# A halo loop that takes its rows in stream order and projects keys and values as tiles arrive

## The chip, the cores and the metric

The kernel runs on all eight cores of one Trainium2 chip. Each core has a TensorE (PE), a VectorE (DVE), a ScalarE (ACT), a GpSimd (POOL) and a SyncE (SP), which work through queues of their own and meet at semaphores. Times are device microseconds of the slowest core. A time is the median of several executions; a profile is one execution on the slowest core.

## What is computed

One decoder layer over 16384 positions of width 1024. Cut to what this change touches:

```python
h = rms_norm(x, g_pre_mix)
proj = h @ w_in                       # q, k, v (768 each), u (256), gates (2048)
q = apply_rope(q); k = apply_rope(k)
# head groups: (window, dilation) = (128, 1), (512, 4), (2048, 16)
outs, lses = [dilated_window_attention(q_g, k_g, v_g, window, dilation) ...]
o_attn = sum(softmax(lses) * outs)
y_pool = multiscale_pool(u, w_pool_mix, pool_scale)   # trailing means over 2, 4, 8, 16
x = x + rms_norm((gate_a * (o_attn @ w_proj_attn) + gate_p * (y_pool @ w_proj_pool)) @ w_out)
x = x + rms_norm((silu(a) * b) @ w_down)              # [a, b] = rms_norm(x) @ w_gate_up
```

In a group of dilation r the positions fall into r streams (position mod r). A query sees the keys of its stream in its own block and in the block before.

## The kernel before

A core owns 2048 positions (16 own tiles of 128, `xo`) and also reads the 2048 positions ahead of them, the **halo** (16 tiles, `xh`), because attention of dilation 16 looks back that far. From the halo the kernel needs keys and values of group 2 (dilation 16) for all 2048 positions, of group 1 for the last 512, of group 0 for the last 128, and u for the last 16.

A tile of x goes through four steps: `t_sq` (ACT squares and sums the row; POOL or ACT and DVE make the reciprocal root), `t_xs` (ACT or DVE scales the row into one of three buffers `xsb`), `t_tr` (PE transposes it in eight 128x128 pieces, DVE writes it out times the gain, into `hTh` for the halo and `hT` for own tiles). A tick of the halo loop (`s_`) squares tile s_, transposes tile s_-3 and scales tile s_-2. `x_load` brings tiles into ten buffers through SP's queue; a load waits for the scaling that frees its buffer. Own tiles have `own_tick`, which does the same steps one tick apart.

`rope_unit` projects keys or queries of a pair of heads for n columns (`proj_fm`: eight matmuls), copies the result to `qb` on ACT, and leaves the rest to the next unit's `rope_flush`: one matmul with `rotm`, two DVE products with the cos and sin tables, one POOL sum into `kT` or `qT`. The tables come by `load_tables`, 512 columns at a time, into two buffers. `v_block` projects 128 positions to values (eight matmuls) and evacuates them. Weights are loaded by POOL's queue (`wload`, `wplan`) and cast to bf16 on the way.

The halo loop has K units of group 2 alone, two for each quarter of the halo (512 positions, `k_halo`). After the loop, in this order: the last quarter's K units, 16 V blocks of group 2 (`v_halo`; stream r reads every 16th column of `hTh`), K and V of group 1, of group 0, and u of the last 16, with an `own_tick` between every few. Then four own blocks of 512 positions follow, each of 12 rope units, with five own ticks in each of the first two and u units in the last two. Then attention starts (line 769 on), and later the gates, the output projection and the FFN.

The code is run straight through by Python; each engine's queue has the order in which the calls stand. There is no scheduler.

## Time and profile before

| | us |
|---|---|
| median of 3 runs | 1005.5 (1005.11 to 1005.79) |
| the profiled execution | 1003.87 |
| its span, slowest core | 1002.3 (cores 998.6 to 1002.3) |
| PE busy | 926.7 (92%) |
| DVE, ACT, POOL busy | 395.6, 343.0, 327.0 |
| mean granted TensorE clock | 0.979 on either die |

The span is the time from the first to the last instruction on the core; the execution has 1.6 us around it. Engine shares are means over stages with different limits, so the stretch that a change touches has to be read by itself, by windows and by the timeline.

### The profile page before, as it was taken

The page shows a single profiled execution, that of the slowest core. Times are in us where ns is not written, and L with a number is a line of the kernel's source. Part 1 is how long each engine was busy: PE and PEld are TensorE (multiplying, and loading weights), DVE is VectorE, ACT ScalarE, POOL GpSimd, SP SyncE. Part 2 cuts the span into 40 slices and gives each one's busy share as a digit, 9 for nine tenths or more (in the row PEclk, how much of TensorE's full clock was granted, in tenths as well). Part 3 has the DMA queues.
Part 4 walks back from the last instruction along what each step waited for, and adds up shares of the span by engine and source line. Part 5 has one row for each costly group of instructions (what it writes and reads, how often), then busy time and mean ns, then how long its engine had stood idle before and what let it go on. Part 6 is the DMA issues. An engine that isn't in the chain of part 4 may idle for free.

```text
span 1002.3 us, 15188 instructions; the slowest of 8 cores (998.6 to 1002.3 us)
## 1 busy us (share of the span) xinstructions
PE 926.7 (92%) x5532; PEld 465.2 (46%) x5532; DVE 395.6 (39%) x556; ACT 343.0 (34%) x580; POOL 327.0 (33%) x318
## 2 busy tenths in 40 slices
PE   1559999999897999999998999999999999999993
PEld 1238554456564444444454444444444444444441
DVE  2466786548887332233687211121112211221111
ACT  4427663349777322223664111110111111111100
POOL 3462787763400333333465111111322000001231
PEclk9779999999999999999999999999999999999997
DMA  8989320000050171112978767663234444430332
GB/s 230 253 186 238 82 64 22 1 1 2 2 86 2 54 115 29 36 22 52 304 273 185 126 111 122 107 118 75 104 126 118 73 84 68 80 63 1 127 110 79
DMA packets 32586, 98.50 MB, mean 98 GB/s; under 512 B 4224, under 2 KB 4224, under 8 KB 32512
## 3 DMA queue, kind: packets, MB, share of 16 engines
q0 software_dynamic: 15296, 41.92, 25.2%
q1 hardware_dynamic: 17072, 55.58, 16.6%
q8 instruction: 45, 0.74, 0.3%
q14 instruction: 29, 0.24, 0.1%
q10 hardware_dynamic: 144, 0.03, 0.0%
HBM read 122.64 MB, written 16.78 MB: 139 GB/s over the span
## 4 chain that ended last, share of the span: by engine, by line
PE 87%; issue 3%; DVE 3%; DMA 2%; ACT 2%; POOL 2%; SPq 0%; DVEq 0%; ACTq 0%; POOLq 0%
PE ps L1194 15%; PE ps L1160 15%; PE ps L1163 14%; PE ps L438 12%; PE ps L934 6%; PE ps L937 6%; PE ps L997 6%; PE ps L518 5%; DMA xst<-xh 2%; PE ps L420 2%; PE ps L944 1%; PE ps L941 1%; PE ps L482 1%; PE ps L791 1%; PE ps L769 1%
## 5 line engine op out<-in xcount | busy, mean ns | idle before, releaser
L1163 PE MATMUL ps<-hT,wgu 128*128 128x512 bf16 x672 | 158.7, 379 | 0.0
L1160 PE MATMUL ps<-hT,wgu 128*128 128x512 bf16 x672 | 158.7, 379 | 0.0
L1194 PE MATMUL ps<-wdn,ffT 128*128 128x512 bf16 x704 | 152.3, 379 | 0.4 <-DMA wdn<-wdn 0.4
L1175 DVE TENSOR_TENSOR ffT<-ps,sa 128x512 bf16<-128x512 f32 x88 | 60.7, 690 | 222.5 <-PE ps L1163 222.5
L1174 ACT ACTIVATE sa<-ps 128x512 f32<-128x512 f32 x88 | 52.5, 597 | 238.8 <-PE ps L1160 238.7
L1194 PEld LDWEIGHTS ps<-wdn,ffT 128*128 128x128 bf16 x704 | 68.8, 98 | 83.7 <-issue 0.8
L1163 PEld LDWEIGHTS ps<-hT,wgu 128*128 128x128 bf16 x672 | 65.7, 98 | 79.3
L1160 PEld LDWEIGHTS ps<-hT,wgu 128*128 128x128 bf16 x672 | 65.6, 98 | 78.6
L74 POOL DMA_DIRECT2D wgu<-wgu x42 | 22.5, 537 | 234.6 <-PE ps L1163 227.5
L438 PE MATMUL ps<-hT,wqk 128*128 128x512 bf16 x384 | 90.5, 379 | 1.2 <-DVE t L485 1.2
L1010 POOL TENSOR_TENSOR x1b<-tb,xin 128x1024 f32<-128x1024 f32 x31 | 72.8, 2348 | 54.4 <-DVE tb L1005 29.6
L956 POOL TENSOR_TENSOR mT<-m,m 128x512 bf16<-128x512 f32 x32 | 40.6, 1268 | 142.9 <-DVE m L951 142.9
L498 POOL TENSOR_TENSOR kT<-t,t2b 128x512 bf16<-128x512 f32 (+1 forms) x36 | 65.6, 1826 | 43.5 <-DVE t2b L487 39.8
L359 ACT ACTIVATE junk<-ps 128x1024 bf16<-128x1024 f32 x31 | 31.5, 1017 | 138.0 <-PE ps L1194 130.8
L1005 DVE SCALAR_TENSOR_TENSOR tb<-ps,rsA,gfin 128x1024 f32<-128x1024 f32 x15 | 19.3, 1284 | 129.5 <-POOL rsA L343 129.5
L508 ACT ACTIVATE qb<-ps 128x512 bf16<-128x512 f32 (+1 forms) x60 | 35.0, 584 | 83.8 <-PE ps L438 82.1
L934 PE MATMUL ps<-hT,wgs 128*128 128x512 bf16 x256 | 62.2, 387 | 0.0
L937 PE MATMUL ps<-hT,wgs 128*128 128x512 bf16 x256 | 60.8, 380 | 0.0
L950 DVE TENSOR_TENSOR m<-ps,sga 128x512 f32<-128x512 f32 x32 | 22.1, 692 | 95.1 <-PE ps L941 91.7
L420 PE MATMUL ps<-ident,xsb 128*128 128x128 bf16 x256 | 23.3, 246 | 38.9 <-ACT xsb L407 20.9
L773 ACT ACTIVATE PT<-ps 128x1024 bf16<-128x1024 f32 x48 | 54.5, 1143 | 12.1 <-PE ps L769 12.1
L438 PEld LDWEIGHTS ps<-hT,wqk 128*128 128x128 bf16 x384 | 37.1, 98 | 44.0 <-issue 1.3
(119 smaller groups left out, 1200.7 us busy)
## 6 DMA issues: line engine op xcount, KB each, us to landing
wgu<-wgu POOLq DMA_DIRECT2D x42, 512.0 KB, 5.2
xst<-xh SPq DMA_DIRECT2D x16, 512.0 KB, 19.1
xin<-xo SPq DMA_DIRECT2D x16, 512.0 KB, 5.4
x1s<-x1b SPq DMA_DIRECT2D x16, 512.0 KB, 3.7
xin<-x1s SPq DMA_DIRECT2D x16, 512.0 KB, 3.9
out<-x1b SPq DMA_DIRECT2D x15, 512.0 KB, 2.9
xst<-xo SPq DMA_DIRECT2D x12, 512.0 KB, 8.6
wdn<-wdn POOLq DMA_DIRECT2D x22, 256.0 KB, 6.0
```

Source lines behind the costliest of these rows:

```text
L438: ev = pe.op(lambda e, k=k: e.matmul(ps[:, bank, 0:n], lhsT=wfn(k), rhs=rhsfn(k), start=(k == 0), stop=(k == 7)), signal=(k == 7))
L498: ev_o = pool.op(lambda e: e.tensor_tensor(out=dst, in0=i0, in1=i1, op=ALU.add), waits=[ev_t1, ev_t2])
L773: ev_e = act.op(lambda e: e.activation(out=PT[k3][:, :, :], in_=ps[:, b0:b0 + 2, :], func=AF.Exp, scale=0.125), waits=[ev, pt_free[k3]])
L934: e1 = pe.op(lambda e, k=k, wb=wb, b1=b1, tok=tok: e.matmul(ps[:, b1, :], lhsT=wgs[wb][:, 0, k, :], rhs=hT[:, k, tok], start=(k == 0), sto ...
L937: e2 = pe.op(lambda e, k=k, wb=wb, b2=b2, tok=tok: e.matmul(ps[:, b2, :], lhsT=wgs[wb][:, 1, k, :], rhs=hT[:, k, tok], start=(k == 0), sto ...
L997: ev = pe.op(lambda e, k=k, hf=hf, pr_=pr_: e.matmul(ps[:, pr_[0] + hf, :], lhsT=mT[:, k, i * 128:(i + 1) * 128], rhs=wout[:, k, hf * 512: ...
L1010: ev_o = pool.op(lambda e: e.tensor_tensor(out=outbuf[:, :], in0=tb[b][:, :], in1=xres[:, :], op=ALU.add), waits=[ev_t, ev_xres, out_free])
L1160: e1 = pe.op(lambda e, k=k, wbuf=wbuf, ba=ba, tok=tok: e.matmul(ps[:, ba, :], lhsT=wbuf[:, 0, k, :], rhs=hT[:, k, tok], start=(k == 0), st ...
L1163: e2 = pe.op(lambda e, k=k, wbuf=wbuf, bb=bb, tok=tok: e.matmul(ps[:, bb, :], lhsT=wbuf[:, 1, k, :], rhs=hT[:, k, tok], start=(k == 0), st ...
L1174: es = act.op(lambda e, ub=ub, ba=ba: e.activation(out=sa[ub][:, :], in_=ps[:, ba, :], func=AF.Silu), waits=[e1, sa_free[ub]])
L1175: ef = dve.op(lambda e, ub=ub, bb=bb, j=j, b=b: e.tensor_tensor(out=ffT[:, j, b * 512:(b + 1) * 512], in0=ps[:, bb, :], in1=sa[ub][:, :], ...
L1194: ev = pe.op(lambda e, j=j, h2=h2, pr_=pr_, il=il: e.matmul(ps[:, pr_[0] + h2, :], lhsT=ffT[:, j, il * 128:(il + 1) * 128], rhs=wdn[:, j, ...
```

## The change

**Halo rows by streams.** The host hands over the halo's 2048 rows permuted, so that tile i holds the 128 positions of stream i (position mod 16 = i), and permutes the cos and sin columns alike. A tile is then one V block of group 2, and four tiles are a K quarter that lies in contiguous runs (`k_stream`, forms -1 to -3 in `rope_flush`).

**Values eight ticks behind.** `v_stream(s_ - 8)` stands in each tick from 8 to 23. The halo's transposed tiles live in a ring of eight, `hTs`, instead of `hTh`; the write of tile i waits for the V block of tile i-8 and for the K units that read its half.

**Last columns kept as runs.** `t_hc` copies the last 32 columns of each tile (its share of the last 512 positions) into `hTc` on ACT. From it come group 1's K and V; `hTd` (last 128) and `hTu` (last 16) are copied from it by ACT after the loop. The keys of those blocks stand in another order, so the first block's masks have their rows permuted alike, and there are four instead of three; a further 512 columns of tables in that order are loaded.

**Four table buffers** instead of two.

**Own ticks.** Own tiles 0 to 3 run in the ticks 16 to 22 of the loop, with the V blocks. Tiles 4 to 15 run in blocks 0 and 1, eight ticks and seven.

**The halo's rest inside the first own block.** K and V of group 1 after unit 3 of block 0, K and V of group 0 after unit 5, u of the last 16 inside block 1. The order of units in blocks 0 to 2 is 10, 11, 8, 9, 6, 7, 4, 5, 2, 3, 0, 1.

**Small ones.** In a tick the scaling stands ahead of the transpose; half of the scalings are on ACT instead of a third; weight loads of wk1 and later stand three ticks and more later; ACT's table is loaded by a one-column square at the start and ACT no longer waits for `cpk`; POOL no longer waits for the end of the halo before the masks.

```diff
@@ t_tr
-        dst, c0 = (hTh, i * 128) if i < NTH else (hT, (i - NTH) * 128)
+        dst, c0 = (hTs, i % 8 * 128) if i < NTH else (hT, (i - NTH) * 128)
...
+            ew = [str_pe.get(i - 8), str_pe.get(("k", i // 4 - 2)), ev_hc.get(i - 8)]
...
+    def t_hc(i):
+        c0, c1 = i % 8 * 128, 128 * (i % 4) + 32 * (i // 4)
+        ev_hc[i] = act.op(lambda e: e.activation(out=hTc[:, :, c1:c1 + 32], in_=hTs[:, :, c0 + 96:c0 + 128], func=AF.Copy), waits=[hev[i]])
...
+    def v_stream(r):
+        c0 = r % 8 * 128
+        v_block(wvr, 2, lambda k: hTs[:, k, c0:c0 + 128], blk_idx(2, r, 0), extra_waits=[wld_ev["wv2"], hev[r]], evac="act" if r % 4 == 0 else "dve")
+        str_pe[r] = pe.last()
...
@@ halo loop
-    for s_ in range(NTH + 3):
+    for s_ in range(NTH + 8):
...
+            if i == 11:
+                tab_own = load_tables(3, HT, 12)
+            if i == 13:
+                tab_n = load_tables(2, HT + T, 4)
+        if 0 <= s_ - 3 < NTH:
+            t_tr(s_ - 3)
+        if 0 <= s_ - 4 < NTH:
+            t_hc(s_ - 4)
+        if 0 <= s_ - 8 < NTH:
+            v_stream(s_ - 8)
+        if 7 <= s_ < 21 and s_ % 4 in (3, 0):
+            k_stream((s_ - 7) // 4, (s_ + 1) % 4)
...
+        if 18 <= s_ < 22:
...
+            x_load(NTH + s_ - 14)
+        if 16 <= s_ < 23:
+            own_tick(0)
+    ev_hd = act.op(lambda e: e.activation(out=hTd[:, :, :].rearrange("p k (r j) -> p k r j", j=8), in_=hTc[:, :, :].rearrange("p k (r j) -> p k r j", j=32)[:, :, :, 24:32],
+                                          func=AF.Copy), waits=[ev_hc[NTH - 1]])
...
@@ own blocks
+    tick_at = {0: (1, 3, 4, 5, 6, 7, 8, 9), 1: (0, 2, 4, 6, 8, 9, 10)}
...
-        order = (6, 10, 7, 11, 8, 9, 0, 4, 1, 5, 2, 3) if b < 3 else (10, 4, 11, 5, 8, 2, 9, 3, 6, 0, 7, 1)
+        order = (10, 11, 8, 9, 6, 7, 4, 5, 2, 3, 0, 1) if b < 3 else (10, 4, 11, 5, 8, 2, 9, 3, 6, 0, 7, 1)
...
+            if b == 0 and n == 3:
+                for pr in range(2):
+                    k_halo(1, pr)
+                for r in range(4):
+                    v_halo(1, r, "dve")
```

How PE's queue changes. Before, in the halo loop from tile 12 on and behind it (the transposes write `hTh`, L438 with `wqk` is a K unit, L482 the product with `rotm`, L518 a V block):

```order
L420 MATMUL ps<-ident_43,xsb_34_76 128x128 x8
L438 MATMUL ps<-hTh_81,wqk_62 128x512 x8
L420 MATMUL ps<-ident_43,xsb_35_77 128x128 x8
L438 MATMUL ps<-hTh_81,wqk_62 128x512 x8
L482 MATMUL ps<-qb_45_87,rotm_44 128x512
L420 MATMUL ps<-ident_43,xsb_36_78 128x128 x8
L482 MATMUL ps<-qb_46_88,rotm_44 128x512
L420 MATMUL ps<-ident_43,xsb_34_76 128x128 x8
L438 MATMUL ps<-hTh_81,wqk_62 128x512 x16
L482 MATMUL ps<-qb_45_87,rotm_44 128x512
L518 MATMUL ps<-wvr_63,hTh_81 128x256 x16
```

Now, from tile 12 on in the loop (L424 is the transpose, L449 the K unit, L538 the V block, L493 the product with `rotm`):

```order
L424 MATMUL ps<-ident_43,xsb_35_77 128x128 x8
L538 MATMUL ps<-wvr_64,hTs_82 128x256 x8
L449 MATMUL ps<-hTs_82,wqk_63 128x512 x8
L424 MATMUL ps<-ident_43,xsb_36_78 128x128 x8
L538 MATMUL ps<-wvr_64,hTs_82 128x256 x8
L449 MATMUL ps<-hTs_82,wqk_63 128x512 x8
L493 MATMUL ps<-qb_52_94,rotm_44 128x512
L424 MATMUL ps<-ident_43,xsb_37_79 128x128 x8
L538 MATMUL ps<-wvr_64,hTs_82 128x256 x8
L493 MATMUL ps<-qb_53_95,rotm_44 128x512
```

Every tick has a V block behind its transpose, which before stood behind the loop.

ACT's queue in own block 0. Before, units without and with a tick take turns (L508 copies qb; L407 scales, L390 squares, L396 takes the root of an own tile):

```order
L508 ACTIVATE qb_45_87<-ps 128x512
L508 ACTIVATE qb_46_88<-ps 128x512
L407 ACTIVATE xsb_36_78<-hTf_82,rsA_50 128x1024
L390 ACTIVATE junk_38_80,ssA_48<-xst_25_67 128x1024
L396 ACTIVATE msA_49<-ssA_48 128x1
L508 ACTIVATE qb_45_87<-ps 128x512
L508 ACTIVATE qb_46_88<-ps 128x512
L407 ACTIVATE xsb_34_76<-xst_24_66,rsA_50 128x1024
```

Now, from unit 6 of block 0 on (L528 copies qb, L411 scales, L394 squares, L400 takes the root):

```order
L528 ACTIVATE qb_52_94<-ps 128x512
L411 ACTIVATE xsb_36_78<-hTf_85,rsA_51 128x1024
L394 ACTIVATE junk_38_80,ssA_49<-xst_25_67 128x1024
L400 ACTIVATE msA_50<-ssA_49 128x1
L528 ACTIVATE qb_53_95<-ps 128x512
L411 ACTIVATE xsb_37_79<-hTf_85,rsA_51 128x1024
L394 ACTIVATE junk_39_81,ssA_49<-xst_26_68 128x1024
L400 ACTIVATE msA_50<-ssA_49 128x1
L528 ACTIVATE qb_52_94<-ps 128x512
```

Each unit there has a scaling, a square and a root behind it, and the next copy of qb stands behind these.

## Rows read from the trace of the kernel before

**Rows 1.** The page, the span in 40 equal slices, busy tenths and granted clock
```profile
PE   1559999999897999999998999999999999999993
...
PEclk9779999999999999999999999999999999999997
```

**Rows 2.** Windows: stretch, its length, busy us per engine (instructions), clock, DMA share, GB/s
```profile
0.00:72.09 72.09, 29.40 (x183) 16.61 (x183) 33.89 (x41) 28.58 (x45) 33.67 (x57) 0.86 0.87 222
72.09:106.70 34.61, 32.98 (x286) 26.41 (x286) 21.80 (x47) 21.74 (x40) 11.84 (x10) 0.94 0.76 195
106.70:218.40 111.70, 111.63 (x578) 53.19 (x579) 74.89 (x118) 50.13 (x86) 86.75 (x53) 1.00 0.14 38
...
40.00:72.09 32.09, 17.96 (x109) 9.78 (x109) 19.10 (x22) 11.26 (x19) 18.96 (x25) 0.71 0.83 180
```

**Rows 3.** Waits from 0 to 72 us: us in total, times, longest
```profile
PE ps L420 <- ACT xsb L407: 20.9, 4, 13.7
...
PE ps L420 <- DVE xsb L409: 18.0, 8, 3.1
```

**Rows 4.** Timeline: start, duration, engine, line, operation, count, [idle before, releaser]
```profile
28.65 3.38 PE L438 MATMUL ps<-hTh,wqk 128*128 128x512 bf16 x8
...
32.31 1.89 PE L438 MATMUL ps<-hTh,wqk 128*128 128x512 bf16 x8
...
39.31 1.06 ACT L390 ACTIVATE junk<-xst 128x1024 bf16<-128x1024 f32 x1 [2.34 <-DMA xst<-xh]
...
47.69 0.60 ACT L508 ACTIVATE qb<-ps 128x512 bf16<-128x512 f32 x1 [5.98 <-PE ps L438]
...
56.79 1.04 ACT L390 ACTIVATE junk<-xst 128x1024 bf16<-128x1024 f32 x1
```

**Rows 5.** Timeline of SP's queue, issues of the loads of x
```profile
14.34 16.91 SPq L74 DMA_DIRECT2D xst<-xh  x6
...
54.83 0.33 SPq L74 DMA_DIRECT2D xst<-xo  x1
```

**Rows 6.** DMA: GB/s in 40 slices of 0 to 70 us, then queues of 0 to 130
```profile
GB/s 0 86 213 248 275 298 260 256 229 174 300 261 290 294 307 274 240 286 352 339 283 323 288 246 249 162 235 105 50 29 110 201 115 238 171 149 272 229 234 232
...
q1 hardware_dynamic: 6704, 19.40, 49.0%
q0 software_dynamic: 3200, 5.74, 26.8%
```

**Rows 7.** Timeline, 86 to 90 us, V blocks, a transpose, and an own tick on ACT
```profile
86.59 2.79 PE L518 MATMUL ps<-wvr,hTh 128*128 128x256 bf16 x24
...
87.00 1.15 ACT L407 ACTIVATE xsb<-xst,rsA 128x1024 bf16<-128x1024 f32 x1
...
88.06 1.04 ACT L390 ACTIVATE junk<-hTf 128x1024 bf16<-128x1024 f32 x1
...
89.22 0.61 PE L420 MATMUL ps<-ident,xsb 128*128 128x128 bf16 x8
89.29 0.20 ACT L396 ACTIVATE msA<-ssA 128x1 f32<-128x1 f32 x1
...
89.67 2.79 PE L518 MATMUL ps<-wvr,hTh 128*128 128x256 bf16 x24
```

**Rows 8.** Groups by line from 0 to 235 us: busy, mean ns, idle before
```profile
L487 DVE TENSOR_TENSOR t2b<-ps,sin 128x512 f32<-128x512 f32 x58 | 40.0, 689 | 28.6 <-PE ps L482 27.7
...
L425 DVE TENSOR_TENSOR hTh<-ps,cpk 128x1024 bf16<-128x1024 bf16 x16 | 19.5, 1223 | 35.7 <-PE ps L420 35.7
...
L524 DVE CAST vA<-ps 128x256 bf16<-128x256 f32 x21 | 8.8, 421 | 5.7 <-PE ps L518 5.7
...
L409 DVE TENSOR_SCALAR xsb<-xst,rsA 128x1024 bf16<-128x1024 f32 x10 | 7.4, 744 | 0.0
```

**Rows 9.** Timeline of PE in own block 0
```profile
112.82 1.89 PE L438 MATMUL ps<-hT,wqk 128*128 128x512 bf16 x8
...
114.76 0.61 PE L420 MATMUL ps<-ident,xsb 128*128 128x128 bf16 x8
```

More of the change, by code:

```diff
@@ L257, in build_program @@
     rotm = P.sb("rotm", [128, 128], BF16, take(256))
-    masks = P.sb("masks", [128, 3, 512], BF16, take(3072))
+    masks = P.sb("masks", [128, 4, 512], BF16, take(4096))
+    hTu = P.sb("hTu", [128, 8, 16], BF16, take(256))
     cpk = P.sb("cpk", [128, 52], F32, take(208))
@@ L366, in build_program @@
     tr_ring = Ring([0, 1])
-    hTh = P.sb("hTh", [128, 8, 2048], BF16, R_Q)
+    hTs = P.sb("hTs", [128, 8, 1024], BF16, R_Q)
+    hTc = P.sb("hTc", [128, 8, 512], BF16, R_Q + 16 * KB)
+    hTd = P.sb("hTd", [128, 8, 128], BF16, R_X + 14 * KB)
+    str_pe = {}
+    ev_hc = {}
     NTH = HT // 128
@@ new lines, in v_stream, with k_halo @@
+    def v_stream(r):
+        c0 = r % 8 * 128
+        v_block(wvr, 2, lambda k: hTs[:, k, c0:c0 + 128], blk_idx(2, r, 0), extra_waits=[wld_ev["wv2"], hev[r]], evac="act" if r % 4 == 0 else "dve")
+        str_pe[r] = pe.last()
+    def k_halo(g, pr):
+        if g:
+            dst = kT[1][:, pr, :].rearrange("p (s L) -> p s L", s=4)[:, :, 0:128]
+            rope_unit(8 + pr, hTc, 512, -2, tab_n, dst, [wld_ev["wk1"], ev_hc[NTH - 1]])
+        else:
+            rope_unit(6 + pr, hTd, 128, -3, tab_n, kT[0][:, pr, 0:128], [wld_ev["wk0"], ev_hd])
@@ new lines, in v_halo, with own_tick @@
+    def v_halo(g, r, evac):
+        fn = (lambda k: hTc[:, k, 128 * r:128 * r + 128]) if g else (lambda k: hTd[:, k, :])
+        v_block(wvr, g, fn, blk_idx(g, r, 0), extra_waits=[wld_ev["wv%d" % g], ev_hc[NTH - 1], ev_hd], evac=evac)
+    own = NTH
+    own_k = [0, 0]
+    def own_tick(batch):
+        k = own_k[batch]
+        own_k[batch] += 1
+        lo, hi = (4, NT) if batch else (0, 4)
+        k += lo
+        if lo <= k - 1 < hi:
+            t_rc(own + k - 1)
+        if lo <= k - 3 < hi:
+            t_tr(own + k - 3)
+        if lo <= k - 2 < hi:
+            n = k - 2
+            t_xs(own + n, n % 2 == 0 or n > 3)
+            if 8 <= n < 12:
+                x_load(own + n + 4)
+        if batch and k < 8:
+            x_load(own + k + 4)
+        if k < hi:
+            t_sq(own + k)
@@ L544, in build_program @@
+    warm = act.op(lambda e: e.activation(out=msA[:, 0:1], in_=nhalf[:, :], func=AF.Square), waits=[ev_ms1])
+    for i in range(6):
         x_load(i)
     tab_h = [load_tables(0, 0, 2)]
-    for i in range(4, NXB):
+    for i in range(6, NXB):
         x_load(i)
     tab_h.append(load_tables(1, 512, 2))
-    wplan = {0: [lambda: load_wk(2)], 1: [lambda: wload("rotm", rotm[:, :], rotm_d[:, :])], 4: [lambda: load_wv(2)],
-             8: [lambda: load_wk(1)], 10: [lambda: load_wk(0)], 12: [lambda: load_wv(1)], 14: [lambda: load_wv(0)],
-             16: [lambda: load_wq(0)], 17: [lambda: load_wq(2)], 18: [lambda: load_wq(1)]}
@@ L624, in build_program @@
-    for f in k0:
-        f()
-    v_halo(0, 0, "dve")
-    own_tick()
-    rope_flush()
-    for c in range(2):
-        k_, bank, ev = proj_fm(lambda k, c=c: wu_t[c][:, k, :], lambda k: hTh[:, k, 2032:2048], 16, [wld_ev["wu"]])
-        ev2 = dve.op(lambda e, c=c, bank=bank: e.tensor_copy(out=uh[:, c, :], in_=ps[:, bank, 0:16]), waits=[ev])
+            if i == 11:
[4 more added lines that the diff above has]
+            t_tr(s_ - 3)
@@ new lines, in build_program @@
+        if 0 <= s_ - 4 < NTH:
[4 more added lines that the diff above has]
+            k_stream((s_ - 7) // 4, (s_ + 1) % 4)
+        if s_ >= 9 and s_ % 4 == 1 and s_ <= 21:
+            rope_flush()
+            if s_ <= 13:
+                tab_h.append(load_tables((s_ - 9) // 4, 1024 + 128 * (s_ - 9), 2))
+        if 18 <= s_ < 22:
+            if s_ == 18:
+                xst_free[NXB:] = [[xsc[t] for t in range(6, NTH)]] * 4
+            x_load(NTH + s_ - 14)
@@ new lines, in build_program @@
+        if 16 <= s_ < 23:
+            own_tick(0)
+    ev_hd = act.op(lambda e: e.activation(out=hTd[:, :, :].rearrange("p k (r j) -> p k r j", j=8), in_=hTc[:, :, :].rearrange("p k (r j) -> p k r j", j=32)[:, :, :, 24:32],
+                                          func=AF.Copy), waits=[ev_hc[NTH - 1]])
+    ev_hu = act.op(lambda e: e.activation(out=hTu[:, :, :].rearrange("p k (q s) -> p k s q", s=4), in_=hTc[:, :, 31:512:32].rearrange("p k (s q) -> p k s q", s=4),
+                                          func=AF.Copy), waits=[ev_hc[NTH - 1]])
@@ L632, in build_program, with u_halo @@
+    def u_halo(c):
+        k_, bank, ev = proj_fm(lambda k: wu_t[c][:, k, :], lambda k: hTu[:, k, :], 16, [wld_ev["wu"], ev_hu])
+        ev2 = dve.op(lambda e: e.tensor_copy(out=uh[:, c, :], in_=ps[:, bank, 0:16]), waits=[ev])
         pj_ring.release(k_, ev2)
         bank_free[bank] = ev2
-    ev_hTh = pe.last()
-    pool.wait(ev_hTh)
     L = 2064
@@ L776, in att_scores @@
         bank_free[b1] = ev_e
-        mv = 2 if g == 2 else (1 if half == 0 and (g == 1 or s_ == 0) else 0)
+        mv = 2 if g == 2 else ((3 if g else 1) if half == 0 and (g or s_ == 0) else 0)
         att_ev[u] = dve.op(lambda e: e.tensor_tensor(out=PT[k3][:, :, :], in0=PT[k3][:, :, :], in1=masks[:, mv, :].unsqueeze(1).to_broadcast([128, 2, 512]),
```

137 lines of the change are left out of this document (54 added, 83 removed).

## The prediction

> **What bounds the kernel now.** I read the page first. TensorE is busy 92% of the span, and the only long hollow stretch is at the start: the PE line opens with 1, 5, 5 tenths while PEclk stands at 9, 7, 7 [rows 1]. The windows say where it ends. Up to 72.1 us PE is busy 29.4 us, with DMA at 0.87; from 72.1 to 106.7 us it is busy 32.98 of 34.61; from 106.7 to 218.4 us, where attention starts, 111.63 of 111.70 us at clock 1.00 [rows 2]. So after 72.1 us the time to 218.4 us is PE work and almost nothing else, and only two things shorten it: to start this dense stretch earlier, or to do part of its work in the hollow before it. Behind 218.4 us nothing is edited that costs time (a fourth mask of the same shape, same instructions), so I carry the end of this phase straight to the end of the kernel.
>
> The hollow has two causes. Until about 39 us the loads lead: ACT's square of halo tile 10 waits for its transfer (39.31) [rows 4]. Behind it no square waits for a transfer; the square of tile 15 runs at 56.79, five tiles in 17.5 us, 3.5 us each. What paces these is the hand-over: PE's transposes wait 20.9 us for xsb from ACT and 18.0 us from DVE [rows 3]. The K projection of a quarter runs its first eight matmuls at the lower clock (3.38 us, the next eight 1.89 us), ACT waits up to 5.98 us for its result (47.69), and the next tile's scaling stands behind that [rows 4]. Loads meanwhile run dry: SP issues the last halo load by 31.2 us and the first own tile only at 54.83 [rows 5], and GB/s falls to 105, 50, 29 around 50 us [rows 6].
>
> **The change, part by part.**
>
> *(a) Sixteen V blocks of dilation 16 move from behind 72.1 us into the halo loop.* The halo rows now come in stream order, so each tile is a complete V block and can be projected eight ticks after its load. Eight matmuls cost 2.63/3 = 0.88 us (86.59 to 89.22, 24 of them) [rows 7]; sixteen are 14.0 us off the dense stretch. The last K quarter (2 units) and own tiles 0 to 3 (4 transposes) also come before the first own block. A unit is 1.94 us (112.82 to 114.76), a transpose 0.45 us (89.22 to 89.67, where the next matmuls start) [rows 7, 9]: 3.9 + 1.8. The halo's rest (K1 2 units 3.9, K0 about 1.3 by its quarter of the columns, 5 V blocks 4.4, the 16-column u pair about 0.5) moves inside block 0 and stays PE work.
>
> *(b) What is left behind the first own matmul.* The stretch 106.7 to 218.4 us keeps its 111.6 us; it holds 10 transposes of own tiles and will hold 12, +0.9; plus 3.9 + 1.3 + 4.4 + 0.5. Sum 122.6 us. The end of the phase is S + 122.6 + stalls, where S is the start of own block 0. Break-even is S = 218.4 - 122.6 - 4 = 92.
>
> *(c) S by the ticks.* A tick holds a square, half an ACT and half a DVE scaling, one transpose with its evacuation, one V block, and on two ticks of four a K unit. DVE: 1.22 + 0.74/2 + 0.42 x 3/4 + 0.69 (half of the two products with the tables, alike) = 2.6 us [rows 8]. ACT: square 1.05 to 1.23, half of 1.06 [rows 7], half of a 0.60 us copy of qb [rows 4], a quarter of 0.42, and the new copy of 32 columns x 8 into hTc. No row shows that copy; it has 256 elements a partition, like the 0.42 us evacuation [rows 8], and a quarter of the 1.15 us scaling [rows 7] would be 0.29. I take 0.4: 2.4 us. PE at the upper clock: 0.45 + 0.88 + 1.94/2 = 2.3 us; at the lower one twice that. So about 2.6 us of the busiest engine, and 2.8 with hand-overs; what was a chain (scale, transpose, K, copy, next scale) has its values three to eight ticks ahead now, which is why I don't take the 3.5 us. Tile 10 cannot come before about 39 us (same bytes ahead of it). Tick 19, nine later, is at 39.3 + 25.2 = 64.5 (at 2.6: 63; at 3.5: 71). Ticks 19 and 20 hold K and V, 3.3 us each, 21 to 23 about 1.5 each: S = 75.6, say **76**.
>
> *(d) S by the loads.* Own tile 3 is needed at tick 19. In the first 130 us SP's queue took 49.0% for 19.40 MB, 3.28 us per MB, and POOL's 26.8% for 5.74 MB, 6.07 us per MB [rows 6]. Ahead of or beside own tile 3 now stand 20 tiles and 5 pairs of tables (13.1 MB, 43 us) and five weight groups (2.6 MB, 16 us): 59 us of engine time, which from a start at 2 to 3 us and with small holes is 62 to 68 us. The loads and the ticks meet; own tiles are issued at tick 12 instead of at 54.83, which fills the hole at 50 us. Two pairs of tables more (own block 0, the extra 512 columns) are in this; the extra pair costs 1.7 us of DMA and stands behind own tile 3.
>
> *(e) Block 0.* Eight ticks for own tiles 4 to 11 stand here, where before five were in a block. A unit with its tick costs ACT 0.60 for qb [rows 4], 1.06 for the scaling, 1.23 for the square and 0.20 for the root, 3.1 us [rows 7], and PE 2.39 us [rows 9]; the transposed product of each unit waits for ACT's qb, so PE can't run ahead. Seven such units in a row are 4.9 us, less what the K0, V0 insert and the first unit's slack give back (about 2.5 us). ACT's two new copies (hTd, 1024 elements, about 1.1 us; hTu) stand before the block's first qb and lie under its first 1.7 us of matmuls. The squares of own tiles 4 to 7 queue behind transfers that are issued at tick 18; if late, ACT stops, and with it qb and PE. I allow **4 us** of stalls in all (1.6 us in the stretch from 72.1 to 106.7 us now [rows 2]).
>
> *(f) Order inside a block* (K2, K1, K0, Q2, Q1, Q0): POOL's heavier sums come four in a row. The last block of before already has such a row and PE has no gap there [rows 2]: nothing. *(g)* The early table load and the dropped wait for cpk start the first square some 2 us sooner, but tile 10 is bound by the loads: nothing.
>
> **Sum.** 76 + 122.6 + 4 = 202.6 us against 218.4: 15.8 us. The profiled execution has span 1002.3 and took 1003.87, 1.6 us under the median of 1005.5. Less 16: span 986.3, that execution 987.9, and on the scale of the median **989.5 us**.
>
> **A rule weighed.** From 40 to 72.1 us the granted clock was 0.71, with PE busy 17.96 of 32.09 us, and from 106.7 us on it was 1.00 [rows 2]. Work in the loop from the first K on is 16 transposes, 16 V, 8 K units = 7.2 + 14.1 + 15.6 = 36.9 us at the upper level; at a mean of 0.71 it would be 52 us, from 28.65 to about 81, five us later than my S. The Trainium skill, "TensorE: Matmul & The Clock Gate", section "What's actually happening", says the default state is throttled and activity releases it. By it the denser loop keeps the upper clock and S stays 76; by the row's mean S would be 81. The second eight matmuls of a quarter at 1.89 us [rows 4] bear the rule out for dense stretches.
>
> **Rivals.**
> 1. *PE stays at the lower clock through the loop (slower).* Gaps between ticks are small but regular. 36.9 us of work then cost 74 us: S = 102, end 102 + 122.6 + 3 = 227.6, 9 us late: 1014.7. It decides against the change from S = 92 on. For it: the lower clock in two slices. Against: PE would be some 80% busy there (36.9 of 47 us) instead of 56%, and the second unit of each pair ran at the upper level even now.
> 2. *Own tiles land late.* If two more weight groups (6.4 us) go ahead and the engines are at 0.87 [rows 2], own tile 3 lands at (59 + 6.4)/0.87 + 2.5 = 78, S = 85, gain 7: 998.5. For it: SP's queue holds everything in order, a table load that waits holds own tiles behind it.
> 3. *ACT sets block 0.* The full 4.9 us, and nearly as much again for squares that wait for tiles 4 to 7: stalls 9, gain 11: 994.5.
> 4. *Better.* Full clock, ticks at 2.6, no stall: S = 70, end 70 + 122.6 + 1 = 193.6, gain 25: 980.7.
> 5. *Nothing gained*: the ticks take 3.5 us and more and rivals 2 and 3 come together, S + stalls near 96: 1005.5.
>
> **How the numbers follow.** Forecast (gain 13 to 19) 0.45, rival 2 0.17, rival 3 0.17, rival 4 0.12, rival 5 0.03, rival 1 0.06. About 0.2% (2 us) is what a measurement of this kernel can tell from no change. Faster 0.91, same 0.03, slower 0.06. The range 982 to 999 takes in rivals 2 and 3 whole and half of rival 4, and leaves out about 0.15.
>
> **What would show it.** Right: the stream's V matmuls stand between 33 and 75 us with the later ones at the upper clock; PE busy in 40 to 72 us rises from about 18 to 25 us or more; the first matmul on own columns at 76 (70 to 82); the phase before attention ends near 203; from there on all as before. Step (c) fails if the squares of tiles 11 to 15 are more than 3.2 us apart; (d) if ACT waits for own tiles at ticks 16 to 19; (e) if PE has more than 5 us of gaps between S and S + 35, behind qb. The whole fails if V blocks in the loop run at twice 0.88 us throughout, or if the first own matmul is later than 92 us.

## The result, and the profile after

| | before | after |
|---|---|---|
| median | 1005.3 us | 997.9 us (996.3 to 1000.6) |
| ratio to before | | 0.9926, 95% interval 0.9903 to 0.9949 |
| span of the profiled execution, slowest core | 1002.3 | 999.0 |
| first matmul of own block 0, median of the cores | (104.8, behind the halo's rest) | 80.5 (79.7 to 81.9) |
| first attention score, median of the cores | 219.1 (217.8 to 221.0) | 211.4 (209.2 to 212.9) |

The kernel is faster by 0.7%, 7.4 us at the medians, where 16 us were forecast. The sign and the mechanism were right; the size was half. A second measurement of the same kernel (e0_again below) gave 996.0 and the ratio 0.9903, a gain of 10 us. Medians, here and below, leave out the executions in which the cores of one die ran at a lower granted clock and took longer.

In what follows, **S** is the start of own block 0's first matmul, **phase** the time from there to the first score matmul of attention, and **tail** the time from there to the end of the core's span. All of them count from the core's own first instruction. On the slowest core of before the first score stands at 221.0, 2.6 us behind the end of the dense stretch in [rows 2], so a phase without stalls is 122.6 + 2.6 = 125.2 us. The kernel after on its slowest core, 7, is S 81.7, phase 131.2, tail 786.1.

The page of after, its two lines of busy tenths and clock, to be laid beside [rows 1]:

```profile
PE   1779899998897999999998999999999999999993
...
PEclk9999999999998999999999999999999999999997
```

The opening 1, 5, 5 has become 1, 7, 7, and the clock's dip to 7 in the second and third slice is gone. The same in windows (columns as in [rows 2]):

```profile
40.00:64.00 24.00, 20.46 (x178) 14.17 (x176) 21.80 (x32) 18.88 (x38) 16.14 (x26) 1.00 0.76 178
64.00:82.00 18.00, 12.86 (x84) 8.15 (x85) 10.95 (x19) 6.93 (x14) 8.14 (x13) 0.81 1.03 254
82.00:116.90 34.90, 32.11 (x196) 17.27 (x194) 20.99 (x39) 18.60 (x36) 18.88 (x16) 0.95 0.62 144
116.90:210.00 93.10, 92.49 (x490) 43.90 (x489) 62.07 (x98) 42.13 (x72) 70.22 (x40) 1.00 0.11 35
...
40.00:72.09 32.09, 25.77 (x211) 16.98 (x209) 23.95 (x37) 21.33 (x43) 17.61 (x28) 1.00 0.83 191
```

Against the same 32 us in [rows 2], PE is busy 25.77 us instead of 17.96, at clock 1.00 instead of 0.71. But from 64 to 82 us there is a new hollow: 5.1 us of PE idle, clock 0.81, and the DMA share is 1.03, the most of any of these windows.

ACT's timeline in that hollow (core 7; squares at L394, of halo tile 15 at 52.35, of own tiles 0 to 3 at 59.25, 60.90, 69.02, 72.68):

```profile
52.35 1.05 ACT L394 ACTIVATE junk<-xst 128x1024 bf16<-128x1024 f32 x1
...
60.90 1.04 ACT L394 ACTIVATE junk<-xst 128x1024 bf16<-128x1024 f32 x1
...
69.02 1.06 ACT L394 ACTIVATE junk<-xst 128x1024 bf16<-128x1024 f32 x1 [4.71 <-DMA xst<-xo]
...
72.68 1.06 ACT L394 ACTIVATE junk<-xst 128x1024 bf16<-128x1024 f32 x1 [1.42 <-DMA xst<-xo]
```

Up to 52.35 the stream runs as forecast (53.3 by the sum). Then own tiles 2 and 3 are not there. Two short windows show that the DMA engines had time for them earlier (share 0.33 and 0.35, the number before the last):

```profile
39.00:43.00 4.00, 2.86 (x33) 2.42 (x33) 4.00 (x6) 3.90 (x9) 3.07 (x4) 1.00 0.33 105
43.00:47.00 4.00, 4.00 (x31) 2.49 (x29) 3.79 (x6) 2.30 (x5) 3.32 (x8) 1.00 0.35 120
```

but SP's queue (issue time, duration) shows that the loads of own tiles 0 and 1, and then of 2 and 3, went out only behind this hole:

```profile
47.73 2.29 SPq L74 DMA_DIRECT2D xst<-xo  x2
50.07 0.42 SPq L74 DMA_DIRECT2D cos<-cost  x1
...
53.60 1.50 SPq L74 DMA_DIRECT2D xst<-xo  x2
```

Two operations that free buffers set these times, on ACT the scaling of halo tile 10 and on DVE a product with a table:

```profile
46.52 1.14 ACT L411 ACTIVATE xsb<-xst,rsA 128x1024 bf16<-128x1024 f32 x1
...
51.60 0.68 DVE L503 TENSOR_TENSOR t2b<-ps,sin 128x512 f32<-128x512 f32 x1
```

Own tile 0 takes the buffer of halo tile 10, and its load is issued when that scaling has ended (47.7 us). The loads of own tiles 2 and 3 stand in SP's queue behind a pair of tables, which is issued at 52.35, when the product has released its buffer. POOL's queue shows what stood beside them, five weight groups of 0.5 MB issued at 45 to 64 us:

```profile
45.44 1.16 POOL L74 DMA_DIRECT2D wqk<-wk  x2
51.69 1.16 POOL L74 DMA_DIRECT2D wqk<-wk  x2
56.39 0.62 POOL L74 DMA_DIRECT2D wvr<-wv  x1
61.41 0.57 POOL L74 DMA_DIRECT2D wvr<-wv  x1
64.36 1.10 POOL L74 DMA_DIRECT2D wqk<-wq  x2
```

PE's timeline, from the wait to the first own block, and then the place in block 0 with group 0's K and V (`hTd`):

```profile
73.04 1.01 PE L424 MATMUL ps<-ident,xsb 128*128 128x128 bf16 x8 [1.26 <-DVE xsb L413]
73.85 1.92 PE L538 MATMUL ps<-wvr,hTs 128*128 128x256 bf16 x8
...
81.68 3.61 PE L449 MATMUL ps<-hT,wqk 128*128 128x512 bf16 x16 [0.60 <-DVE hT L432]
...
102.86 0.38 PE L493 MATMUL ps<-qb,rotm 128*128 128x512 bf16 x1 [0.87 <-ACT qb L528]
...
105.40 0.22 PE L493 MATMUL ps<-qb,rotm 128*128 128x128 bf16 x1 [1.72 <-ACT qb L528]
105.63 1.51 PE L538 MATMUL ps<-wvr,hTd 128*128 128x256 bf16 x8
106.93 3.14 PE L449 MATMUL ps<-hT,wqk 128*128 128x512 bf16 x8
```

These waits are paid twice: behind them a transpose takes 1.01 us instead of 0.61, a V block 1.92 instead of 1.04, a K unit's eight matmuls 3.14 instead of 1.89, wholly or in part at the lower of TensorE's two clocks (1.2 instead of 2.4 GHz).

The third place is far behind the change, at the start of the output projection. The cores come in pairs (0 and 1, 2 and 3, and so on). In the kernel after, the one of a pair that begins the output projection later (each by the time since its own first instruction) has the longer tail in all four pairs: 785.1 against 780.0, 783.8 against 780.5, 783.8 against 780.8, 786.1 against 780.2 us. The waits of POOL there, from 455 to 520 us (us in total, times, longest), on core 7 and then on its partner 6:

```profile
POOL x1b L1045 <- DMA xin<-xo: 7.8, 2, 4.8
```
```profile
POOL x1b L1045 <- DMA xin<-xo: 2.9, 2, 1.6
```

`xin` are the rows of x that the output projection adds back (line 1045, one sum `x1b` on POOL for each of 16 tiles). On core 7 they come late: the third sum ends 23.2 us behind the core's first output projection matmul, on core 6 18.3 us, and the last one 77.2 against 74.1 us. PE on core 7 waits for the outcome at the start of the FFN, and then for the FFN's own `ffT`; on core 6 it has only the second wait:

```profile
527.67 0.61 PE L1096 MATMUL ps<-ident,xs 128*128 128x128 bf16 x8 [1.93 <-DVE xs L1084]
529.51 3.45 PE L1195 MATMUL ps<-hT,wgub 128*128 128x512 bf16 x8 [1.23 <-DVE ffT L1210]
```
```profile
523.83 1.89 PE L1195 MATMUL ps<-hT,wgub 128*128 128x512 bf16 x8 [1.08 <-DVE ffT L1210]
```

The matmuls behind the two waits take 3.45 us, those behind the single one 1.89. From its first output projection matmul to its first FFN matmul with weights loaded in the FFN itself (`wgu`; the first two groups are `wgub`) core 7 takes 81.3 us and core 6 76.6. I call this the **burst stretch**.

The tail of core 7, 786.1, is 4.8 us longer than the 781.3 of the slowest core of before. Of these, 2.4 us are in the burst stretch (81.3 against 78.9), 1.0 between the first score and the output projection, and 1.4 behind the stretch. Only the first part is followed up below; the causes of the other two are open.

### The profile page after: what moved, and what is told of

Read it like the earlier page. It is cut to its first block, busy times and chain, and to the rows that moved or that the text cites. A ratio compares the mean times of both kernels' runs of the same rounds, so it can differ in the third digit from the quotient of the medians.

```text
span 999.0 us, 15229 instructions; the slowest of 8 cores (989.2 to 999.0 us)
## 1 busy us (share of the span) xinstructions
PE 926.5 (93%) x5532; PEld 462.5 (46%) x5532; DVE 394.0 (39%) x552; ACT 350.3 (35%) x603; POOL 320.1 (32%) x318
## 4 chain that ended last, share of the span: by engine, by line
PE 80%; DMA 6%; ACT 4%; issue 4%; DVE 3%; POOL 2%; SPq 1%; DVEq 0%; ACTq 0%; POOLq 0%
PE ps L1229 15%; PE ps L1195 15%; PE ps L1198 15%; PE ps L449 10%; PE ps L969 6%; PE ps L972 6%; PE ps L538 5%; DMA xst<-xh 2%; DMA xin<-xo 2%; DMA xst<-xo 2%; PE ps L979 1%; PE ps L976 1%; PE ps L826 1%; PE ps L804 1%; POOL x1b L1045 1%
## 5 line engine op out<-in xcount | busy, mean ns | idle before, releaser
L449 PE MATMUL ps<-hT,wqk 128*128 128x512 bf16 x384 | 91.6, 383 | 0.6 <-DVE hT L432 0.6
L518 POOL TENSOR_TENSOR kT<-t,t2b 128x512 bf16<-128x512 f32 (+1 forms) x36 | 57.5, 1612 | 42.3 <-DVE t2b L503 36.9
L528 ACT ACTIVATE qb<-ps 128x512 bf16<-128x512 f32 (+1 forms) x60 | 34.9, 584 | 67.8 <-PE ps L449 61.3
L449 PEld LDWEIGHTS ps<-hT,wqk 128*128 128x128 bf16 x384 | 37.3, 99 | 43.6 <-issue 2.5
L1032 PE MATMUL ps<-wout,mT 128*128 128x512 bf16 x256 | 56.9, 379 | 0.0
```

What stands on the lines that cost most here:

```text
L449: ev = pe.op(lambda e, k=k: e.matmul(ps[:, bank, 0:n], lhsT=wfn(k), rhs=rhsfn(k), start=(k == 0), stop=(k == 7)), signal=(k == 7))
L518: ev_o = pool.op(lambda e: e.tensor_tensor(out=dst, in0=i0, in1=i1, op=ALU.add), waits=[ev_t1, ev_t2])
L1032: ev = pe.op(lambda e, k=k, hf=hf, pr_=pr_: e.matmul(ps[:, pr_[0] + hf, :], lhsT=mT[:, k, i * 128:(i + 1) * 128], rhs=wout[:, k, hf * 512: ...
```

## The experiments

All use the kernel after as their base, except e9. Ratios are to the kernel before on the same chip, where its median was between 1005.3 and 1006.5. S and attention start are medians over eight cores of one profile, the late tail is the mean over the four cores that begin the output projection later than their partner.

| run | median us | ratio (95% interval) | S | attention | late tail |
|---|---|---|---|---|---|
| before | 1005.3 | 1 | | 219.1 | 782.0 |
| after | 997.9 | 0.9926 (0.9903 to 0.9949) | 80.5 | 211.4 | 784.7 |
| e0_again | 996.0 | 0.9903 (0.9878 to 0.9927) | 79.8 | 210.1 | 782.0 |
| e1_weights_late | 991.9 | 0.9862 (0.9841 to 0.9884) | 75.6 | 206.4 | 782.8 |
| e2_v_one_eighth | 996.7 | 0.9908 (0.9885 to 0.9931) | 79.5 | 211.1 | 782.3 |
| e3_v_double | 997.7 | 0.9909 (0.9882 to 0.9936) | 82.2 | 212.2 | 783.5 |
| e4_ticks_off_k0 | 995.4 | 0.9902 (0.9877 to 0.9927) | 80.1 | 208.8 | 783.2 |
| e5_weights_and_ticks | 991.2 | 0.9861 (0.9838 to 0.9885) | 75.6 | 204.8 | 782.5 |
| e6_late_weights_v_eighth | 996.2 | 0.9898 (0.9873 to 0.9923) | 77.0 | 208.4 | 782.8 |
| e7_boot_later | 988.1 | 0.9819 (0.9799 to 0.9839) | 75.6 | 204.8 | 780.2 |
| e8_tables_late | 998.0 | 0.9913 (0.9891 to 0.9935) | 78.2 | 212.2 | 781.4 |
| e9_before_boot_later | 1003.9 | 0.9976 (0.9963 to 0.9989) | | 219.1 | 780.7 |
| e10_after_boot_later | 995.1 | 0.9883 (0.9864 to 0.9903) | 79.4 | 209.6 | 780.7 |
| e11_all_and_tables | 990.0 | 0.9831 (0.9809 to 0.9853) | 75.5 | 204.7 | 781.2 |

An interval is about 2.3 us to either side, so only differences of 3 us and more between two rows are to be read in time; smaller ones only in the profile.

**Weights later (e1_weights_late).** My theory was that the weight groups take the DMA engines from own tiles 2 and 3.

```diff
-             11: [lambda: load_wk(1)], 13: [lambda: load_wk(0)], 15: [lambda: load_wv(1)], 17: [lambda: load_wv(0)],
-             19: [lambda: load_wq(2)], 21: [lambda: load_wq(1)], 23: [lambda: load_wq(0)]}
+             17: [lambda: load_wk(1)], 19: [lambda: load_wv(1)], 20: [lambda: load_wk(0)], 21: [lambda: load_wv(0)],
+             22: [lambda: load_wq(2)], 23: [lambda: load_wq(1), lambda: load_wq(0)]}
```

> The five weight groups wk1, wk0, wv1, wv0, wq2 are issued later (ticks 17 to 23), behind the own tiles. Theory LOADS (the first own matmul is late because own tiles 2 and 3 compete with weights on the same DMA engines): ACT's waits for own tiles (4.7 and 1.4 us in the changed kernel) shrink by 3 us or more, the first own matmul moves from 80 to 82 us to 76 to 78, attention starts at 206 to 209 instead of 209 to 213, time 3 to 5 us under the changed kernel (993 to 995). Theory COMPUTE (the loop's own work sets it): the first own matmul stays at 80 to 82 and the time at 997 to 999. If weights now come too late for block 0, PE waits for wk1 or wv1 and the time is over 999.

S moved from 80 to 75.6, attention from about 211 to 206.4, the time by 4 to 6 us, all a little more than expected. ACT's timeline, the squares of own tiles 2 and 3 (slowest core, 3):

```profile
63.72 1.04 ACT L394 ACTIVATE junk<-xst 128x1024 bf16<-128x1024 f32 x1
...
66.32 1.05 ACT L394 ACTIVATE junk<-xst 128x1024 bf16<-128x1024 f32 x1
```

Neither waits any more. All that ACT waits for between 50 and 78 us is K units (3.8 us) and one root (0.5 us). It is shown that the weights on POOL's queue delayed S by 4 to 5 us. They don't stand in SP's queue, and they delayed its loads all the same. The Trainium skill, "DMA: Bandwidth & Descriptors", section "Issuing engines are not separate DMA queues", says that loads of different engines run on the same 16 DMA engines and interleave; this run agrees, with 4.7 and 1.4 us of waiting that went when the other queue's loads did.

**V work taken away or doubled (e2_v_one_eighth, e3_v_double).** Is the V work in the loop really hidden, as part (a) says?

```diff
-        for k in range(8):
-            ev = pe.op(lambda e, k=k: e.matmul(ps[:, bank, 0:256], lhsT=tok_ap_fn(k), rhs=wv_tile[:, 2 - g, k, :], start=(k == 0), stop=(k == 7)),
-                       signal=(k == 7))
+        for k in range(nk):
+            ev = pe.op(lambda e, k=k: e.matmul(ps[:, bank, 0:256], lhsT=tok_ap_fn(k % 8), rhs=wv_tile[:, 2 - g, k % 8, :], start=(k == 0), stop=(k == nk - 1)),
+                       signal=(k == nk - 1))
```

with `nk` 1 in the first and 16 in the second (the eight products taken twice) for the V blocks of the stream, 8 for all others.

> Each of the 16 V blocks in the halo loop has one matmul instead of eight (values of the halo's dilation-16 group are wrong, seven eighths of their PE work, 12.3 us, is left out). LOADS: that work is hidden under the loads, the first own matmul moves by less than 1.5 us and the time stays within 2 us of the changed kernel (996 to 999). COMPUTE: PE is the loop's bound, the first own matmul comes 4 us or more earlier, time 992 to 994.

> Each V block in the halo loop of the changed kernel is done twice over (16 matmuls, 14 us of PE work more; values of the halo's dilation-16 group are doubled and so wrong). If the V work were free under the loads at any amount, the time would not move. From the trace PE has no gap of more than 1.5 us between 33.9 and 64 us, so LOADS says: the slack before own tile 3 lands is some 8 us, the rest shows: first own matmul 4 to 8 us later, time 1002 to 1006. Rival, PE is the loop's bound already: all 14 us show, time 1010 to 1014.

Seven eighths of 14 us of PE work gone: no gain that can be measured. 14 us more of it: S 2 us later and no loss that can be measured, where I had expected 4 to 8 us. On core 5 the doubled version squares own tiles 2 and 3 at 67.15 and 70.48 us without a wait for their loads, and after at 67.73 and 72.12 with waits of 4.45 and 2.16 us: PE's extra work went into time that ended in a wait otherwise. The windows on core 5 from 40 to 64 us, of after, of the doubled and of the cut version:

```profile
40.00:64.00 24.00, 20.55 (x176) 14.25 (x177) 21.66 (x33) 18.16 (x36) 16.37 (x26) 1.00 0.82 189
```
```profile
40.00:64.00 24.00, 24.00 (x215) 18.45 (x213) 17.81 (x25) 15.71 (x32) 13.56 (x22) 1.00 0.75 184
```
```profile
40.00:64.00 24.00, 17.65 (x109) 9.14 (x107) 19.15 (x28) 16.86 (x34) 14.44 (x23) 0.78 0.83 185
```

Doubled, PE is busy all 24 us at clock 1.00. Cut, it holds 109 matmuls instead of 176 and is still busy 17.65 us, because the clock is 0.78. Taking work from PE there lowers its clock, and the K units pay for it. The Trainium skill, "TensorE: Matmul & The Clock Gate", section "What's actually happening", says that activity releases the throttle; the three windows agree.

**Both (e6_late_weights_v_eighth).** The same cut with the late weights, to see whether the V blocks set S once the loads don't.

> Late weights and, in the same kernel, V blocks of one matmul (values of the halo's dilation-16 group wrong). With the transfers out of the way PE's work in the loop should be the next bound: the first own matmul goes from 75.6 us to 70 to 73, where the same omission without late weights gave 1.0 us. Time 987 to 989. Rival: something else holds the loop (ACT or DVE, or the landing of own tile 3 still): first own matmul within 1.5 us of 75.6, time 990 to 992.

Neither outcome came. S is 77.0 and attention 208.4, later than with the whole V work (75.6 and 206.4), and the time is 996.2 against 991.9. Of these 4 us 2.0 are there at attention; where the others are lost is not shown. The granted clock of core 5 from 40 to 64 us is 0.86, in e1 1.00. PE's timeline on core 5 has a K unit at the lower clock behind a wait:

```profile
61.76 3.57 PE L449 MATMUL ps<-hTs,wqk 128*128 128x512 bf16 x8 [3.02 <-DVE hTs L432]
```

So the 14 us of V work in the loop cost nothing, and here leaving most of them out cost time.

**Ticks of block 0 (e4_ticks_off_k0, e5_weights_and_ticks).** In after, own ticks stand beside group 0's short K units, where PE waits for ACT's `qb`.

```diff
-    tick_at = {0: (1, 3, 4, 5, 6, 7, 8, 9), 1: (0, 2, 4, 6, 8, 9, 10)}
+    tick_at = {0: (1, 3, 6, 7, 8, 9, 10, 11), 1: (0, 2, 4, 6, 8, 9, 10)}
```

> The own ticks of block 0 move from units 1,3,4,5,6,7,8,9 to units 1,3,6,7,8,9,10,11, so none stands right before the small K0 units. Theory ACT (K0's two units give PE only 0.44 us each to cover 3.1 us of ACT, and the gaps drop PE's clock): the gaps before L493 behind qb in block 0 (0.9 + 1.7 us, and some 2 us of matmuls at the lower clock behind them) go, attention starts 3 to 5 us earlier than in the changed kernel with the first own matmul unmoved, time 993 to 995. Rival: the stalls only move to units 6 to 11, where ACT's 3.1 us per unit stands against PE's 2.4: attention start within 1.5 us, time 996 to 999.

> Both edits, late weights and ticks off K0. If both theories hold and add: first own matmul at 76 to 78, attention at 203 to 206, time 989 to 992. If only one holds, 993 to 995. If the lost time returns later (the stage of output projection and first FFN half took 2 to 5 us more on the core that is behind its neighbour), attention moves as said but the time less, 992 to 996.

The phase, 129.4 to 131.2 us on the cores of after, is 128.6 to 128.9 in e4. Attention starts some 2 us earlier, where I had expected 3 to 5. PE's timeline there (slowest core, 0), to be laid beside the rows at 102.86 to 106.93 above:

```profile
102.20 0.38 PE L493 MATMUL ps<-qb,rotm 128*128 128x512 bf16 x1 [0.28 <-ACT qb L528]
...
103.12 1.03 PE L538 MATMUL ps<-wvr,hTd 128*128 128x256 bf16 x8
103.99 1.89 PE L449 MATMUL ps<-hT,wqk 128*128 128x512 bf16 x8
```

The waits of 0.87 and 1.72 us are one of 0.28, and the lower clock behind them is gone. That is shown for the phase. In the time nothing of the 2 us is seen: 0.9902 alone against 0.9903 of the same kernel without it (e0_again, below), 0.9861 against 0.9862 on top of the late weights. These differences are below what the intervals can tell, and in e4 the slowest core's tail is 785.7; whether the 2 us were lost there or only not resolved stays open.

**The same kernel again (e0_again).**

> The changed kernel unaltered, once more on this chip, as the base for its neighbours. Both theories: 996 to 1000, first own matmul 80 to 82 us, attention 209 to 213.

996.0, with late tails of 782.0 on average where the first profile had 784.7. The loss in the tail differs from execution to execution.

**The gate weights' first loads later (e7_boot_later).** If the tail's loss is a shortage of memory bandwidth when a pair of cores starts the output projection, then whatever in this burst isn't needed yet should go later. `wgu_boot` (two loads of 0.5 MB) is first used by the FFN, 60 us later. The base is e5.

```diff
-    boot_ev = [pool.dma(wgu_boot[i][:, :, :, :], wgu_d[i], d_gub[i]) for i in range(2)]
+    boot_ev = []
...
     for it in range(NT):
+        if it == 6:
+            boot_ev += [pool.dma(wgu_boot[i][:, :, :, :], wgu_d[i], d_gub[i]) for i in range(2)]
         wout_step(it)
```

> Late weights, ticks off K0, and the two FFN weight loads that stand at the start of the output projection are issued six tiles later. Theory PAIR: at that point the core that is behind its neighbour has its first x tiles delayed by these loads of both cores (POOL waited 4.8 and 3.0 us for them on core 7, 1.6 and 1.3 on core 6), and pays 2 to 5 us behind attention. Then the stretch from attention to the end becomes 779 to 781 on all cores (781.6 median, up to 784.1 in the kernel without this edit), the slowest core is at 984 to 986, time 986 to 988. Rival: the delay comes from later (down projection weights, stores of x1): unchanged, 991 to 992.5.

988.1 us, 3 us below e5 by the medians and 4 by the ratios, with attention starting at the same 204.8; the tails of all eight cores are 779.1 to 781.0, and the burst stretch is 76.6 to 76.9 us on all of them (76.7 to 80.8 in e5). On core 6, the later of its pair here, `xin` is not among the waits of POOL from 455 to 520 us; on core 7 it is

```profile
POOL x1b L1045 <- DMA xin<-xo: 1.6, 1, 1.6
```

It is the fastest kernel of the study and beats both, by 1.8% and about 1%.

**The same edit alone, on either kernel (e9_before_boot_later, e10_after_boot_later).**

> The kernel before, with only the two first gate weight loads (1 MB together) issued at the seventh step of the output projection instead of ahead of it; nothing is left out. Theory P (a core that is a little behind its partner finds the memory taken by the partner's burst at the start of the output projection, and these 1 MB are the part of the burst nobody needs yet): the tails of before, 779.5 to 782.5 us, come together near 779 to 780, the slowest core gains 1 to 2 us, 1003.5 to 1005.5. Theory Q (the burst costs only in the kernel after, whose cores reach it closer together): nothing, 1005 to 1006.5. The gain is to be smaller than the 4 us that the same edit gave on top of the later weights and ticks.

> The kernel after, with only the two first gate weight loads issued at the seventh step of the output projection; nothing is left out. Theory P (the tail of the slowest core, 783.8 to 786.1 us against 780.2 to 780.8 of its partner, is this burst): all tails at 779 to 781, time 992 to 993.5, 4 us under the kernel after. Theory Q (the 4 us of the earlier run came from something that the later weights and ticks made possible): less than 1.5 us, 995 to 997, and tails of 784 and more on the core that comes second.

On the kernel before it gains 0.24% (1.1 to 3.7 us). The loss was there already: core 1 of before waited 10.3 us for `xin`, longest 4.7, and in this run no wait for `xin` is among POOL's six longest on core 0, the later core of that pair here. On the kernel after the ratio falls from 0.9926 and 0.9903 to 0.9883, 4 us against the first measurement of it, which is clear of the intervals, and 2 us against the second, which is not; late tails are 780.7 on average instead of 784.7 and 782.0. POOL's waits of before (core 1), then of e10 on its slowest core, 5:

```profile
POOL x1b L1010 <- DMA xin<-xo: 10.3, 3, 4.7
```
```profile
POOL x1b L1045 <- DMA xin<-xo: 1.4, 1, 1.4
```

For the kernel before, theory Q (nothing) falls, since the interval leaves out a ratio of 1. For the kernel after, the time of 995.1 lies in Q's range (995 to 997) and not in P's (992 to 993.5); it is the profiles that speak for P. Over the ten with the early loads the later core of a pair has the longer tail in 37 of 40 pairs, by 1.1 to 4.3 us on average; over the four with the later loads in 14 of 16, by 0.9 to 2.0 us. The burst stretch is plainer. With the early loads it is longer on the later core in all 40 pairs, 77.6 to 81.5 us against 76.6 to 77.5 on the partner; with the later loads it is 76.6 to 77.0 us on all 32 cores. POOL's third sum ends 21.0 to 23.2 us behind the first output projection matmul on the later cores of the ten profiles, and 16.2 us on all 32 of the four. So it is shown that the two loads cost the later core its time in this stretch, and that the edit ends this. The 0.9 to 2.0 us that are left between the tails of a pair are not lost there, and their cause is open. Nor is a wait for `xin` by itself the loss: core 0 of e11 waits 6.5 us for its first rows, and its burst stretch is 76.9 us.

The Trainium skill, "HBM Reference", section "Specifications (TRN2)", says that the two cores of a domain share its bandwidth; the pairs in the trace agree, but no run here had a core alone, and no trace puts the two cores of a pair on one scale of time. So that it is this sharing, and not something else that a pair has in common, is likely and not shown.

**Tables behind own tiles 2 and 3 (e8_tables_late, e11_all_and_tables).** SP's queue has two pairs of tables (0.5 MB each) between the loads of own tiles 0, 1 and those of 2, 3, and a third behind these. What part have they in the late own tiles? The edit puts one of the two behind own tiles 2 and 3 and the third behind the four `hTf` loads.

```diff
-            if i == 11:
-                tab_own = load_tables(3, HT, 12)
-            if i == 13:
-                tab_n = load_tables(2, HT + T, 4)
+            if i == 14:
+                tab_own = load_tables(3, HT, 12)
...
+        if s_ == 21:
+            tab_n = load_tables(2, HT + T, 4)
```

> The kernel after with the two last pairs of tables (1 MB) issued behind own tiles 2 and 3 (the last one behind the four hTf loads) instead of ahead of them; nothing is left out. Theory A (what makes own tiles 2 and 3 land at 69.0 and 72.7 us is the weights on POOL's queue, as the run with later weights said): the tables are 3 us of engine time and their move gains little; first own matmul 79 to 81 us, time as the kernel after (996 to 998). Theory B (the tables ahead of them on SP's own queue hold them up as much as the weights did): own tiles 2 and 3 are issued 3 us earlier and land 3 to 4 us earlier, first own matmul 77, time 993 to 995. A third outcome: the own block's first products now wait for their table, and the gain is given back behind the first own matmul.

> Later weights, block 0's ticks moved back, the gate weights later, and the tables behind own tiles 2 and 3; nothing is left out. Once the weights are later no square waits for an own tile, so by theory A the tables' move gives nothing more: first own matmul 75 to 76, 988. By theory B the ticks run up to 1 us earlier: 74.5, 987. Slower than 989 if the first own product waits for its table.

The third outcome of e8 came true. ACT's squares of own tiles 2 and 3 stand at 65.96 and 70.95 (core 0), where after had 69.02 and 72.68 (core 7), S is 78.2, but the phase is 132.8 to 136.3 us, and attention starts no earlier. DVE's product with the table of group 1's keys shows where it went:

```profile
65.96 1.06 ACT L394 ACTIVATE junk<-xst 128x1024 bf16<-128x1024 f32 x1 [3.14 <-DMA xst<-xo]
...
70.95 1.06 ACT L394 ACTIVATE junk<-xst 128x1024 bf16<-128x1024 f32 x1 [2.75 <-DMA xst<-xo]
```
```profile
95.15 0.69 DVE L501 TENSOR_TENSOR t<-ps,cos 128x512 f32<-128x512 f32 x1 [5.13 <-DMA sin<-sint]
```

The extra pair of tables for the halo's last columns now lands last, 5.1 us after it is wanted. With the weights later too (e11), nothing waits for either, S and attention are those of e7, and the time can't be told from e7's, though it is 2 to 3 us above what I had expected. So the tables ahead of own tiles had a part of about 2 us in S, the weights about 4, and of the two edits only moving the weights carried its gain to attention.

## Why the prediction was off, step by step

The steps that failed are (d), the landing of own tile 3, and the step that carried the end of the phase straight to the end of the kernel; (e) was too small. The profiled execution was forecast with span 986.3 and has 999.0: 12.7 us. They fall into three parts: S 81.7 instead of 76 (5.7), the phase 131.2 instead of 125.2 + 4 (2.0), and the tail 786.1 instead of the 781.3 of before (4.8); 0.2 is rounding. At the medians the miss is smaller, 997.9 or 996.0 against 989.5, mainly since the tail's part differs between executions.

- **(a) right.** PE is busy 25.8 us of the 32 at clock 1.00, and they are free: e2 and e3.
- **(b) right.** From 116.9 us on PE is busy 92.49 of 93.10 us; no work has come or gone unforeseen.
- **(c) right.** The square of tile 10 stands at 39.25 (39.3 forecast), that of tile 15 at 52.35 (53.3), the last four ticks 2.7 us apart (2.8). The new copy into `hTc` took 0.41 us (0.4). With the loads out of the way e1 had S at 75.6 against my 76. One reading behind it was loose: of the 39 us that the transposes waited for `xsb` up to 72 us [rows 3], 25.5 lie before 40 us, where the loads lead, and only 13.5 in the stretch of which I said that the hand-over paces it.
- **(d) wrong, and the largest miss.** The sum itself gave 62 to 68 us for own tile 3; it is 72.7. It failed in two terms. The first is the hole in the loads. I let it be filled because own tiles are issued at tick 12. They are, but that tick comes at 47.7 us, since own tile 0 waits for the scaling of halo tile 10, and own tiles 2 and 3 come only at 53.6, behind tables that wait for a buffer. So the 16 engines stood two thirds idle from 39 to 47 us (share 0.33 and 0.35), 5.3 us that the sum had as small holes. The second is the weights. The queues from 0 to 73 us on core 7 (packets, MB, share of the 16 engines):

```profile
q1 hardware_dynamic: 4411, 13.29, 58.3%
q0 software_dynamic: 1697, 3.44, 28.7%
```

  SP's 42.6 us are the 43 of the sum, but POOL's are 21 instead of 16: not five weight groups but seven had been issued before own tile 3 landed. Rival 2 had both, the two more groups and the tables that hold own tiles behind them, with S = 85 and so too long a price. That its time, 998.5, is near the measured 997.9 is chance, since its S is 4 us late and it has nothing for the tail. e1 shows the part of the weights, e8 the smaller one of the tables; no run filled the hole, so its part is an estimate.
- **(e) right place, too small.** Stalls in the phase are 6.0 us instead of 4, and 2 of them are two waits for `qb` at group 0's K units with the lower clock behind them. I had priced ACT's 3.1 us against PE's 2.39, and had not priced that 128-column units have only 0.61 us of matmuls apiece while ACT's tick is the same. e4 took these 2 us out of the phase. By the sign that I had given (over 5 us of gaps from S to S + 35) the step did not fail: there are 2.8 us from 82.0 to 116.9.
- **"I carry the end of this phase straight to the end": wrong.** Nothing behind attention was edited, and yet the gain of 8.1 us at the first score (221.0 to 212.9) is 3.3 us at the end of the span (1002.3 to 999.0). I had put a difference behind attention at nothing, for the reason that the program there is the same. It was 4.8 us. The 2.4 us of them in the burst stretch are shown by e7, e9 and e10 to hang on two loads; the kernel before had this loss too (78.9 us on its slowest core, 76.7 on the partner, and a 10.3 us wait for `xin` on core 1), and I didn't look for it, since I read only the stretch that the change touches. The other 2.4 us are open. In e0_again, the same kernel, the late tails are 2.7 us shorter, so a part of the 4.8 belongs to this one execution.
- **(f), (g) right.** The rows of POOL's heavier sums cost PE nothing: it is busy 92.49 of 93.10 us in blocks that have the new order. ACT's earlier table load gave nothing that shows either; tile 10 is at 39.25, where before it stood at 39.31 [rows 4].
- **A rule weighed.** The clock stayed at 1.00 from 40 to 72 us, as by the rule and not as by the row's mean of 0.71. Rival 1 is refuted, and with it the case of a slower kernel. The clock did fall behind the waits for own tiles: it is 0.50 from 72.09 to 76.70 us on core 7. In e1, without these waits, it is 0.82 there (core 3), behind a wait of 2.48 us for `xsb`, so they are the larger part of the fall and not all of it.

With the weights of (d), (e) and the burst mended (e7) the kernel is at 988.1. That this is near the forecast 989.5 is in part chance: e7 also removes a loss that the kernel before had, and the forecast had left in.
